# Transposing the attention probabilities by VectorE blocks and a DRAM scratch instead of TensorE transposes

## The reference, cut to what matters

```python
h = rms_norm(x, pre_mix_g)
u, gate_b, gate_c, c_q, c_kv, k_rope = split(h @ w_in)          # 3 x 1024, 768, 512, 64 columns
y_conv = group_rms_norm(gate_b * conv3(gate_c * u), 8 groups)
q = rms_norm(c_q) @ w_uq ; kv = rms_norm(c_kv) @ w_ukv          # 8 heads: 128 nope + 64 rope, 128 v
s = (q_nope @ k_nope.T + rope(q_rope) @ rope(k_rope).T) * scale # two blocks of 128 queries;
p = softmax(where(chunk mask, s, -1e30))                        # block 0 sees 128 keys, block 1 sees 256
o = p @ v                                                       # then rms-normed per head
x = x + rms_norm(concat(y_conv, o) @ w_o)
x = x + rms_norm(relu(rms_norm(x) @ w_up)**2 @ w_down)
```

## Time and profile before

| | |
|---|---|
| median of 3 runs | 1067.26 us (1067.23 to 1068.05) |
| the profiled execution, its own time | 1067.39 us |
| its span, from the first to the last instruction | 1065.6 us |
| mean granted TensorE clock | 0.997 |
| TensorE busy (matmuls) | 1053.6 us, 99% |
| VectorE, ScalarE busy | 695.2 us, 515.9 us |
| DMA over the span | 225.78 MB, 212 GB/s |

### The profile page before, as it was taken

One profiled execution on the slowest core, in us unless ns is written; L12 is line 12 of the kernel. 1 busy time (PEld: TensorE's weight loads), 2 busy tenths in 40 slices (PEclk: granted clock), 3 DMA queues, 4 the chain that ended last, 5 costly groups with the idle time before them and its releaser, 6 DMA issues.

```text
span 1065.6 us, 13494 instructions
## 1 busy us (share of the span) xinstructions
PE 1053.6 (99%) x4794; PEld 877.0 (82%) x4794; DVE 695.2 (65%) x785; ACT 515.9 (48%) x666; POOL 80.7 (8%) x94
## 2 busy tenths in 40 slices
PE   9999999999999999999999999999999999999996
PEld 7898888888888788888888888888888888888885
DVE  6475566679975876575575665756657656565666
ACT  7575545565544664444444444444444444444443
POOL 0011022110000310000000000000000000000003
PEclk9999999999999999999999999999999999999998
DMA  9786667864586465776666756666576665676562
GB/s 345 261 300 218 201 184 272 271 221 151 204 307 198 125 212 157 237 226 197 209 184 212 231 172 232 196 199 212 170 236 216 203 211 159 220 232 190 181 242 79
DMA packets 125619, 225.78 MB, mean 212 GB/s; under 512 B 8464, under 2 KB 30096, under 8 KB 124816
## 3 DMA queue, kind: packets, MB, share of 16 engines
q1 hardware_dynamic: 125152, 224.89, 64.7%
q10 hardware_dynamic: 432, 0.44, 0.1%
HBM read 210.08 MB, written 7.34 MB: 204 GB/s over the span
## 4 chain that ended last, share of the span: by engine, by line
PE 85%; issue 11%; DVE 2%; POOL 1%; DMA 1%; ACT 0%; SPq 0%; DVEq 0%; POOLq 0%; ACTq 0%
PE ps L725 28%; PE ps L727 28%; PE ps L726 28%; DMA raw<-in_w_in 1%; PE ps L748 1%; POOL acc L1666 0%; DVE w_lo L1305 0%; PE ps L909 0%; PE ps L914 0%; POOL x_res L1777 0%; POOL x_res L1751 0%; ACT w_hi L1005 0%; SPq L656 0%; DVE conv_s L1532 0%; DVEq L311 0%
## 5 line engine op out<-in xcount | busy, mean ns | idle before, releaser
L1305 DVE TENSOR_TENSOR w_lo<-raw,w_hi 128x1024 fp32r<-128x1024 f32 (+2 forms) x382 | 465.2, 1226 | 318.9 <-ACT w_hi L1005 316.8
L1005 ACT ACTIVATE w_hi<-raw 128x1024 fp32r<-128x1024 f32 (+2 forms) x382 | 395.8, 1038 | 460.7 <-PE ps L727 456.3
L725 PE MATMUL ps<-w_hi,xT_hi 128*128 128x512 f32 (+1 forms) x792 | 308.5, 390 | 0.6 <-DVE xT_lo L1406 0.5
L727 PE MATMUL ps<-w_lo,xT_hi 128*128 128x512 f32 (+1 forms) x792 | 305.9, 386 | 0.0
L726 PE MATMUL ps<-w_hi,xT_lo 128*128 128x512 f32 (+1 forms) x792 | 305.8, 386 | 0.0
L725 PE MATMUL ps<-w_hi,yT_hi 128*128 128x512 f32 x672 | 263.1, 391 | 0.0
L727 PE MATMUL ps<-w_lo,yT_hi 128*128 128x512 f32 x672 | 261.6, 389 | 0.0
L726 PE MATMUL ps<-w_hi,yT_lo 128*128 128x512 f32 x672 | 261.4, 389 | 0.0
L725 PEld LDWEIGHTS ps<-w_hi,xT_hi 128*128 128x128 f32 x792 | 148.7, 188 | 31.9 <-issue 2.0
L727 PEld LDWEIGHTS ps<-w_lo,xT_hi 128*128 128x128 f32 x792 | 148.6, 188 | 30.0
L726 PEld LDWEIGHTS ps<-w_hi,xT_lo 128*128 128x128 f32 x792 | 148.8, 188 | 28.7
(11 more groups left out here) (155 smaller groups left out, 425.3 us busy)
## 6 DMA issues: line engine op xcount, KB each, us to landing
raw<-in_w_up SPq DMA_DIRECT2D x64, 1024.0 KB, 5.5
raw<-in_w_down SPq DMA_DIRECT2D x64, 1024.0 KB, 5.3
raw<-in_w_in SPq DMA_DIRECT2D x28, 1024.0 KB, 6.0
raw<-in_w_o SPq DMA_DIRECT2D x16, 1024.0 KB, 5.0
aT_raw<-a_blk SPq DMA_DIRECT2D x240, 32.0 KB, 1.9
raw<-in_w_uq SPq DMA_DIRECT2D x8, 576.0 KB, 4.9
mix_rows<-blk SPq DMA_DIRECT2D x32, 128.0 KB, 2.4
raw<-in_w_ukv SPq DMA_DIRECT2D x4, 1024.0 KB, 5.3
```

The lines of the kernel that those rows point to most:

```text
L725: nc.tensor.matmul(dst, x_hi, hi, start=first, stop=False)
L727: mm = nc.tensor.matmul(dst, x_hi, lo, start=False, stop=last)
L1005: nc.scalar.activation(w_hi[:, slot, 0:size], raw[:, raw_slot, first:first + size], ACT.Copy).then_inc(hi_ready, 1)
L1305: nc.vector.tensor_tensor(w_lo[:, slot, 0:size], raw[:, raw_slot, first:first + size], f32(w_hi[:, slot, 0:size]), ALU.subtract).then_inc( ...
```

## The change

The probabilities of a pair are no longer transposed by TensorE.

- `probs_turn` (`at` 18): VectorE transposes all of `probs` (128 x 768) in 32 x 32 blocks into the memory of `probsT`.
- `probs_store` (20): ScalarE's queue issues four DMAs to a new scratch `probs_rows` in DRAM, 96 KB each.
- `probs_read` (23): ScalarE's queue waits for the four and issues one DMA of 384 KB back into `probs`.
- `probs_order` (26): ScalarE waits for it and copies the 128 x 768 into the order of `probsT`.
- `pv` moves from 22 to 28, and what follows it by the same six chunks: the norm steps to 30 and 31, the turn of the result to 32, its split to 42. 28 is `at` 12 of the next pair, where `qrT` now stands (it was 9).
- The transposes of `probsT` on TensorE and both PSUM copies are gone.
- The first eight quads of the output product are taken in another order, so that the second half of the attention result is used four chunks later; their number and size are unchanged.

```diff
--- before.py
+++ after.py
@@ -149,11 +149,12 @@
                 steps.append(("q_out", p, n))
             if at == 6:
                 turn("kq", p)
-            if at == 26:
+            if at == 32:
                 turn("o", p)
-            for when, what, h in [(9, "qrT", 0), (13, "q_order", 0), (15, "scores", 0), (15, "scores", 1),
-                                  (19, "probsT", 0), (19, "probsT", 1), (22, "pv", 0), (24, "o_squares", 0),
-                                  (25, "o_norm", 0), (36, "o_split", 0)]:
+            for when, what, h in [(12, "qrT", 0), (13, "q_order", 0), (15, "scores", 0), (15, "scores", 1),
+                                  (18, "probs_turn", 0), (20, "probs_store", 0), (23, "probs_read", 0),
+                                  (26, "probs_order", 0), (28, "pv", 0), (30, "o_squares", 0), (31, "o_norm", 0),
+                                  (42, "o_split", 0)]:
                 if at == when:
                     steps.append((what, p, h))
         for c in range(4):
@@ -179,7 +180,7 @@
         steps.append(("conv_out", i, n))
 
 
-    order = [(0, 2), (0, 3), (0, 0), (1, 2), (1, 3), (1, 0), (0, 1), (1, 1)]
+    order = [(s, q) for q in (2, 3, 0, 1) for s in (0, 1)]
     order += [(s, q) for s in (2, 3) for q in (2, 3, 0, 1)]
     for s, q in order:
         n = quad("out", strip=S_OUT + s, q=q, nk=4, width=W, col=s * W, first=q == 2, last=q == 1)
@@ -421,7 +422,8 @@
         qT_ready = sem("qT_ready")
         qrT_filled, qrT_ready = sem("qrT_filled"), sem("qrT_ready")
         scores_done, neg_max_ready, probs_ready = sem("scores_done"), sem("neg_max_ready"), sem("probs_ready")
-        probsT_filled, probsT0_ready, probsT1_ready = sem("probsT_filled"), sem("probsT0_ready"), sem("probsT1_ready")
+        probs_turned, probs_stored, probs_landed = sem("probs_turned"), sem("probs_stored"), sem("probs_landed")
+        probsT_ready = sem("probsT_ready")
         pv_done, o_ready, o_sq_ready = sem("pv_done"), sem("o_ready"), sem("o_sq_ready")
         ss_o_ready, rstd_o_ready, o_normed = sem("ss_o_ready"), sem("rstd_o_ready"), sem("o_normed")
         oT_hi_ready, oT_lo_ready = sem("oT_hi_ready"), sem("oT_lo_ready")
@@ -509,6 +511,8 @@
             k = m - Q_RANK // P
             return yT_hi[:, KV_AT + k], yT_lo[:, KV_AT + k], G_KV + k
 
+        probs_rows = nc.dram_tensor("probs_rows", (4, BLK, 4, 6 * BLK), F32, kind="Internal").ap()
+        probs_blk = probsT.rearrange("p h n -> p (h n)").rearrange("p (q c i) -> p q c i", q=4, c=6)
         mix_rows = nc.dram_tensor("mix_rows", (4, BLK, 4, 8 * BLK), F32, kind="Internal").ap()
 
         def landed(batch):
@@ -901,7 +905,7 @@
                     if p:
 
                         pe.wait_ge(o_ready, p)
-                        pe.wait_ge(probsT1_ready, p)
+                        pe.wait_ge(probs_ready, 2 * p)
                     parts = [(0, slice(0, P), slice(0, P)), (1, slice(P, 3 * P), slice(0, SEQ))]
                     for h in range(2):
                         for tb, cols, keys in parts:
@@ -915,16 +919,11 @@
                                                   krT[rp, keys], start=False, stop=True, skip_group_check=True)
                             if tb:
                                 mm.then_inc(scores_done, 1)
-                elif what == "probsT":
-                    pe.wait_ge(probs_ready, 2 * a + b + 1)
-                    transposes((6, 7)[b], [probs[:, b, i * P:(i + 1) * P] for i in range(3)]
-                               ).then_inc(probsT_filled, 1)
                 elif what == "pv":
                     pe.wait_ge(kv0_ready, a + 1)
                     pe.wait_ge(kv1_ready, a + 1)
-                    pe.wait_ge(probsT0_ready, a + 1)
-
-                    pe.wait_ge(probsT1_ready, a + 1)
+                    pe.wait_ge(probsT_ready, a + 1)
+                    pe.wait_ge(probs_ready, 2 * a + 2)
                     for h in range(2):
                         o = [ps[:, 6, (2 * h + tb) * P:(2 * h + tb + 1) * P] for tb in range(TB)]
                         v = [v_sb[:, a % 2, tb, h] for tb in range(TB)]
@@ -950,7 +949,7 @@
                     pe.wait_ge(conv_sq_ready, i + 1)
                     if i == 0:
 
-                        pe.wait_ge(probsT1_ready, PAIRS)
+                        pe.wait_ge(probs_ready, 2 * PAIRS)
                     elif a == 0:
 
                         pe.wait_ge(conv_std_ready, b)
@@ -1143,18 +1142,30 @@
                     act.wait_ge(neg_max_ready, i + 1)
                     if a:
 
-                        act.wait_ge(probsT_filled, i - 1)
+                        act.wait_ge(probsT_ready, a)
                     bank = (6, 7)[b]
                     for tb, cols in [(0, slice(0, P)), (1, slice(P, 3 * P))]:
                         s = 2 * b + tb
                         ins = nc.scalar.activation(probs[:, b, cols], ps[:, bank, cols], ACT.Exp, scale=SCALE,
                                                    bias=neg_max[:, s:s + 1], accum_out=row_sum[:, s:s + 1])
                     ins.then_inc(probs_ready, 1)
-                elif what == "probsT" and b == 1:
-                    act.wait_ge(probsT_filled, 2 * a + 2)
+                elif what == "probs_store":
+                    act.wait_ge(probs_turned, a + 1)
                     if a:
-                        act.wait_ge(pv_done, a)
-                    nc.scalar.activation(probsT[:, 1], ps[:, 7, 0:3 * P], ACT.Copy).then_inc(probsT1_ready, 1)
+                        act.wait_ge(probs_landed, 16 * a)
+                    for g in range(4):
+                        act.dma_start(probs_rows[:, :, g].rearrange("q r n -> r q n"),
+                                      probs_blk[BLK * g:BLK * (g + 1)].rearrange("p q c i -> p q (c i)")
+                                      ).then_inc(probs_stored, 16)
+                elif what == "probs_read":
+                    act.wait_ge(probs_stored, 64 * (a + 1))
+                    act.dma_start(probs.rearrange("p h n -> p (h n)"), probs_rows.rearrange("q r g n -> (q r) (g n)")
+                                  ).then_inc(probs_landed, 16)
+                elif what == "probs_order":
+                    act.wait_ge(probs_landed, 16 * (a + 1))
+                    nc.scalar.activation(probsT.rearrange("p h n -> p (h n)").rearrange("p (c g i) -> p g c i", c=6, g=4),
+                                         probs.rearrange("p h n -> p (h n)").rearrange("p (g c i) -> p g c i", g=4, c=6),
+                                         ACT.Copy).then_inc(probsT_ready, 1)
                 elif what == "o_split":
                     act.wait_ge(blk_landed, landed(("o", a)))
                     for h in range(2):
@@ -1476,12 +1487,14 @@
                     own(nc.vector.reduce_max(row_max[:, s + 1:s + 2], ps[:, bank, P:3 * P], AX_X))
                     nc.vector.tensor_scalar(neg_max[:, s:s + 2], row_max[:, s:s + 2], -SCALE, None,
                                             ALU.mult).then_inc(neg_max_ready, 1)
-                elif what == "probsT" and b == 0:
-                    dve.wait_ge(probsT_filled, 2 * a + 1)
+                elif what == "probs_turn":
+                    dve.wait_ge(probs_ready, 2 * a + 2)
                     if a:
 
                         dve.wait_ge(pv_done, a)
-                    nc.vector.tensor_copy(probsT[:, 0], ps[:, 6, 0:3 * P]).then_inc(probsT0_ready, 1)
+                    nc.vector.transpose(probs_blk.rearrange("p q c i -> p c q i"),
+                                        probs.rearrange("p h n -> p (h n)").rearrange("p (c q i) -> p c q i", c=6, q=4)
+                                        ).then_inc(probs_turned, 1)
                 elif what == "pv":
                     dve.wait_ge(probs_ready, 2 * a + 2)
                     own(nc.vector.reciprocal(inv_sum[:], row_sum[:]))
```

## The result

The changed kernel takes 1077.68 us (median of four executions, 1076.26 to 1078.16) where the kernel before took 1067.29 beside it (1067.23 to 1068.05). The ratio is 1.0092, 95% interval 1.008 to 1.0105: 10.4 us slower. The forecast was 1067.6 us with a range up to 1069.8, so it was wrong. The rival that called the direction, C, had 0.20. All medians in this document are of executions near full clock; one of the version "pair 4 by TensorE", 1784 us at a mean granted clock of 0.557, is left out.

The account below looks back on a forecast made before the run. TensorE was taken as the bound, at full clock and never waiting between 90 and 300 us. Terms: -2.64 + 0.3 + 0.3 + 2.4 = +0.4 us, giving 1067.6 us; range 1064.5 to 1069.8.

Parts of the forecast that it names:

- Rival C: Scratch reads land late everywhere; from 6.5 us of landing waits exceed 4.7 us, at 8 us 1073.6 us; chance 0.20.
- The transposes' 0.66 us per pair: TensorE's queue: six transposes and the change back to weight products, 0.66 us per pair, 2.64 us for four.
- The 0.3 us of `o_split` ahead of the copy: ScalarE's queue, pairs 2 and 3: `o_split` ahead of `probs_order` makes TensorE wait 0.3 us in each.
- Pair 1's spare: At pair 1's `pv`: operand ready after 2.24 us, TensorE arrives after 2.72, so 0.5 us to spare.
- The chain through pair 4: Pair 4: read out at 240.7, landing 245.4, copy, `pv` can start at 246.6; TensorE, there at 244.2, waits 2.4 us.
- VectorE's turn of 768 columns: `probs_turn` on VectorE: 1.05 us, estimated from 0.70 us for a turn of 512 columns.
- One step that failed: SP's queue: the next weight load is held some 8 us longer behind merged turns; taken as 0, at most 0.5 us.
- The other step that failed: Read to copy, pairs 1 to 3: 6.4 us of lead, 7.2 behind `o_split`, hides the 4.7 us landing.
- All three values: Landing of the 384 KB read: 3.3, 4.7 (taken) or 6.2 us, all claimed hidden in pairs 1 to 3.
- the 4.6 us that the prediction estimated: Read's landing when sharing DMA engines with SP's queue: 2.0 us fixed, 1.3 us of moving doubled, 4.6 us in all.

Follow-up runs that it names:

- pair 4 by TensorE: The changed kernel with only the last pair's probabilities transposed by TensorE as before: 1072.2 us against 1067.55, ratio 1.0041.
- no scratch: The changed kernel without the four stores and the read; VectorE's turn and ScalarE's copy stay: 1068.91 us against 1067.59, ratio 1.0014.
- traffic only: The kernel before, its transposes kept, plus the scratch's stores and read on ScalarE's queue: 1068.02 us against 1067.59, ratio 1.0005.
- the last version: The changed kernel respaced, conv turns at 34 and 50, pair 4 transposed by TensorE; no new TensorE waits: 1065.82 us against 1067.72, ratio 0.9983.
- long pause: The kernel before with TensorE made to wait in the MLP for a 2048-column GpSimd product: 1073.84 us, ratio 1.0055.
- turn at 34: The changed kernel with the turn of the result at 34 instead of 32: 1076.47 us against 1067.59, ratio 1.0091.
- read at 21: The changed kernel with turn at 17, stores at 18 and read at 21: 1073.91 us against 1067.55, ratio 1.0062.
- conv turns early: The changed kernel with the convolution's turns at chunks 34 and 50 instead of 38 and 54: 1075.56 us against 1067.67, ratio 1.0072.
- best guess: The changed kernel respaced, conv turns at 34 and 50, result's turn at 33, second half's `conv_norm` two chunks later: 1071.76 us against 1067.67, ratio 1.0037.
- short pause: The kernel before with TensorE made to wait in the MLP for a 1024-column GpSimd product: 1071.85 us against 1067.67, ratio 1.004.
- moves and traffic: The kernel before with the moves, stores and read, TensorE's transposes kept, `pv` not waiting for the read: 1073.91 us against 1067.72, ratio 1.0063.

## Why the prediction was wrong

**Right.** The transposes' 0.66 us per pair: the ledger above closes with 2.64 to within 0.4 us, and the version without waits wins 2.0 us for three pairs. The 0.3 us of `o_split` ahead of the copy: 0.33 in "no scratch". Pair 1's spare: no wait. The chain through pair 4 in kind: read out, landing, copy, `pv`. VectorE's turn of 768 columns took 0.97 us (estimated 1.05).

**One step that failed** is in the part on what is hidden and reads "SP now finds `conv_turn` and `o_turn` of pairs 1 and 2 behind the same weight load ... I take 0, at most 0.5 us", together with what isn't there: the turn of keys and queries on the same queues, which the new traffic and the moved turns together delay. The hold did reach ScalarE, which waited 3.0 and 4.3 us for raw weights, and so the reads that it issues. The margin of the keys of 1.3 to 1.5 us stood in the trace of before (landing of `kqT` against the start of the scores) and was not read. The scores' waits are 3.2 us of the sum, where the prediction has 0.

**The other step that failed**, and the larger one, is the overlap: "the read goes out with the split after chunk 21, the copy is due after the split behind chunk 25", so "All three values are hidden in pairs 1 to 3". The landing, taken as 4.7 us, was mis-sized as well: the median was 6.2 us, the reads of pairs 2 to 4 took 5.9 to 6.9. But that alone would have been hidden; what was missing is the lead. ScalarE's timeline of the changed kernel around pair 3:

```profile
213.53 0.34 ACTq L1162 DMA_DIRECT2D probs<-probs_rows  x1
...
217.51 0.91 ACT L1173 ACTIVATE yT_hi<-lat,gains 128x256 fp32r<-128x256 f32 x2
219.42 0.84 ACT L1166 ACTIVATE probsT_sb<-probs 128x768 f32<-128x768 f32 x1 [1.00 <-DMA probs<-probs_rows]
```

The read is issued at 213.53, the copy starts at 219.42 after 1.00 us of pure waiting behind `o_split`, and TensorE was at `pv` at 218.67. From read to `pv` the plan has six chunks, 8.2 us. It was 7.95 us in pair 1, 6.5 in pair 2, 5.1 in pair 3 and 2.8 in pair 4, since ScalarE, which issues the read, had itself been stopped (4.26 us for raw weights just before pair 3's), while TensorE went on with halves that were split already. Less 1.07 us for copy and weight load, 5.5, 4.1 and 1.7 us were left for landings of 6.9, 5.9 and 6.1: waits of 1.4, 1.8 and 4.4, the measured ones to within 0.1 us. With the read two chunks earlier they were 0.33, 0.33 and 0.6.

**Pair 4** was forecast with 2.4 us and took 4.47. The read's issue was forecast 3.5 us ahead of TensorE's arrival (240.7, 244.2) and came 2.8 ahead (246.32, 249.1): 0.7 us. The landing took 6.1 us instead of 4.7: 1.4 us. Together 2.1, the whole miss. The order of the steps in the chain was right.

**Not thought of:** the clock, 1.4 to 1.7 us behind the longest wait.

By terms: forecast -2.64, +0.6 in pairs 2 and 3, +2.4 in pair 4, sum +0.4. Measured -2.64, +3.3 at `pv` in pairs 2 and 3, +3.2 at the scores, +4.5 at `pv` in pair 4, +1.4 to 1.7 of clock, and 0.3 to 0.6 left for small gaps: +10.3. Rival C named the right wait for less than two thirds of the loss, and had the direction in part by luck: it was priced by landings from 6.5 us on, which one read of four reached (6.9), and would have needed 9 us to come to +10.

The prediction weighed the Trainium skill (DMA: Bandwidth & Descriptors, Queues, rings and completion order), by which a DMA engine takes turns between its queues packet by packet, for the new read alone. No run isolates how the queues share. The reads took 5.9 to 6.9 us in the changed kernel and 5.0 to 6.5 in "traffic only", all longer than the 4.6 us that the prediction estimated with that page's fixed 2.0 us, a figure that the page fits to DMAs issued from GpSimd. The Trainium skill's rule (VectorE: DVE Perf Modes, Rules for kernel authors), TensorE for a 128 x 128 transpose, agrees with the result of this change as it stands: 0.66 us of TensorE against a way through DRAM that was spaced out over 15.4 us from stores to copy in pair 1 (123.64 to 139.04), on shared queues. The last version shows that it isn't the whole answer, since there three pairs gain by that way.

## What to carry to other kernels

Before adding a transfer or moving one, list every dependent transfer on the same queues with its margin, from the landing to the moment its consumer comes: a margin of 1.3 us looks like "never waits" in the profile, and two changes that each fit into it cost nearly nothing alone and 6 us together. Compare what slowed down with a version that has the moves but not the traffic before blaming the traffic: the weight loads took 7.4 us without it and 7.8 with it. A detour through DRAM has to be timed from its issue when the issuing engine is itself behind, not from the plan. Where most places gain and one loses, try the change without that one: here it was the difference between 1.0025 and 0.9983. And a wait of some microseconds put into a saturated TensorE can cost more than its length: 1.7 us more behind one of 3.7 us.

## What the runs showed of the hardware

- Behind a wait of TensorE the granted clock was 0.5 for 3.4 us: after idle times of 4.3 us (changed kernel), 3.7 us (long pause), 2.7 and 2.4 us (turn at 34), 2.7 us (read at 21) and 2.2 us (pair 4 by TensorE). With the conv turns early it was 0.5 for 6.8 us, beginning 1.4 us before the end of a wait of 4.3 us. It was not behind 2.0 us in the changed kernel and 3.2 us at 300 us in "best guess". Which waits it follows was not settled, and it differs between executions of one kernel: with the short pause as told above, and in "moves and traffic" executions at a mean clock of 0.998 took 1071.7 and 1072.4 us, those at 0.994 1076.2 and 1076.5.
- In the changed kernel the scratch's DMAs landed in 1.8 us at best; the 96 KB stores took 5.0 us as a median and the 384 KB reads 5.9 to 6.9 us. In the last version the stores took 3.6 us, with the same SP traffic spread out, and the reads 5.9 to 6.6.
- A DRAM tensor that is only declared went with a slower read of another one: the 512 KB `kqT` read of pair 1 took 3.2 to 3.3 us in four kernels without `probs_rows` and 3.7 to 4.1 in thirteen with it, before the first DMA to it.
- Four DMA issues in a row on ScalarE took 2.97 us in pair 1 and 1.77 to 2.2 us in the others (taken: 1.77). Such an issue can take 1.42 us by itself (309 ns at least, median 456).
